# Moving four gate tiles of a two-block transformer kernel into the loop of its recurrent mixer

## The reference, cut to what matters

```python
u = rms_norm_2(h, g_norm_mix[l])
proj = u @ w_in[l] + b_in[l]
mq, mk, mv, mo, mi, mf, nq, nkv, ngate, merge = split_columns(proj, IN_SIZES)
y_m = mlstm_mixer(mq, mk, mv, mo, mi, mf, ...)     # 4 heads x 4 chunks of 128 tokens, recurrent
y_n = nsa_mixer(nq, nkv, ngate, ...)               # compressed, selected and windowed attention
ys = jnp.stack([y_m, y_n], axis=2)
branch = jnp.einsum('btnw,nwd->btnd', ys, w_branch[l])
gates = jax.nn.sigmoid(merge.reshape(B, T, N_BRANCH, D_MODEL))
mixed = jnp.sum(gates * branch, axis=2)            # gate_0 * (y_m @ W_0) + gate_1 * (y_n @ W_1)
h = h + mixed @ w_out[l]
```

## Time and profile before

| | us |
|---|---|
| Time, median of 3 runs (2259.81 to 2261.11) | 2260.12 |
| Profiled execution: its own time | 2263.99 |
| Profiled execution: span of its instructions | 2262.7 |
| TensorE busy, of the span | 2133.4 (94%) |
| VectorE busy | 988.6 (44%) |
| ScalarE busy | 815.3 (36%) |
| GpSimd busy | 226.7 (10%) |
| Mean granted clock of TensorE | 0.979 |

### The profile page before, as it was taken

One profiled execution on the slowest core, in us unless ns is written; L12 is line 12 of the kernel. 1 busy time (PEld: TensorE's weight loads), 2 busy tenths in 40 slices (PEclk: granted clock), 3 DMA queues, 4 the chain that ended last, 5 costly groups with the idle time before them and its releaser, 6 DMA issues. The chain is left out here.

```text
span 2262.7 us, 25574 instructions
## 1 busy us (share of the span) xinstructions
PE 2133.4 (94%) x10364; PEld 1712.6 (76%) x10364; DVE 988.6 (44%) x1833; ACT 815.3 (36%) x1574; POOL 226.7 (10%) x256
## 2 busy tenths in 40 slices
PE   6899899999998999999999999988898999999997
PEld 5667688888887767688888877767665788888886
DVE  6265453323336364453323346645355444333333
ACT  4145443223224355342222334342355434222222
POOL 3003410000000004210000000000254201000000
PEclk9899999999999999999999999989899999999999
DMA  6521123233332312123333222313411232323321
GB/s 154 109 75 57 57 80 106 89 98 103 93 98 71 94 47 75 62 84 97 98 98 93 98 80 75 93 29 84 103 48 38 61 117 84 102 89 101 100 89 69
DMA packets 273721, 192.10 MB, mean 85 GB/s; under 512 B 22060, under 2 KB 241364, under 8 KB 273604
## 3 DMA queue, kind: packets, MB, share of 16 engines
q1 hardware_dynamic: 268704, 177.76, 27.3%
q0 software_dynamic: 4752, 12.67, 2.5%
q10 hardware_dynamic: 148, 0.04, 0.0%
HBM read 186.21 MB, written 4.23 MB: 84 GB/s over the span
## 5 line engine op out<-in xcount | busy, mean ns | idle before, releaser
L584 PE MATMUL bank<-h_features,weights_hi_lo 128*128 128x512 f32 (+1 forms) x5160 | 1138.2, 381 | 17.1 <-DVE weights_hi_lo L917 7.9
L584 PEld LDWEIGHTS bank<-h_features,weights_hi_lo 128*128 128x128 f32 x5160 | 933.7, 190 | 206.7 <-issue 14.6
L917 DVE TENSOR_TENSOR weights_hi_lo<-weights,weights_hi_lo 128x1024 fp32r<-128x1024 f32 (+1 forms) x337 | 402.7, 1199 | 703.7 <-ACT weights_hi_lo L1521 703.1
L1521 ACT ACTIVATE weights_hi_lo<-weights 128x1024 fp32r<-128x1024 f32 (+1 forms) x337 | 340.9, 1016 | 401.2 <-PE bank L626 352.4
L624 PE MATMUL bank<-weights_hi_lo,hidden 128*128 128x512 f32 x528 | 205.4, 389 | 0.0
L625 PE MATMUL bank<-weights_hi_lo,hidden 128*128 128x512 f32 x528 | 205.4, 389 | 0.0
L626 PE MATMUL bank<-weights_hi_lo,hidden 128*128 128x512 f32 x528 | 205.4, 389 | 0.0
L1637 ACT ACTIVATE hidden<-arena 128x512 fp32r<-128x512 f32 x66 | 41.7, 632 | 300.0 <-DVE arena L1068 300.0
L1930 POOL TENSOR_SCALAR arena<-arena,row_stats 128x256 f32<-128x256 f32 (+5 forms) x140 | 126.3, 913 | 198.7 <-DVE row_stats L992 70.9
L1902 POOL TENSOR_TENSOR h_features<-arena,h_features 128x512 fp32r<-128x512 f32 x24 | 30.7, 1278 | 992.0 <-ACT h_features L1549 992.0
L1068 DVE TENSOR_TENSOR arena<-bank,arena 128x512 f32<-128x512 f32 x66 | 45.6, 692 | 181.3 <-PE bank L584 181.3
(11 more groups left out here) (335 smaller groups left out, 2063.8 us busy)
## 6 DMA issues: line engine op xcount, KB each, us to landing
weights<-in_w_in_dram SPq DMA_DIRECT2D x84, 512.0 KB, 3.9
weights<-in_w_gate_dram SPq DMA_DIRECT2D x66, 512.0 KB, 3.8
weights<-in_w_up_dram SPq DMA_DIRECT2D x66, 512.0 KB, 3.8
weights<-in_w_down_dram SPq DMA_DIRECT2D x60, 512.0 KB, 3.6
weights<-in_w_out_dram SPq DMA_DIRECT2D x24, 512.0 KB, 3.7
bias_rows<-decay_scratch POOLq DMA_DIRECT2D x16, 256.0 KB, 4.0
weights<-in_w_cmp_dram SPq DMA_DIRECT2D x16, 256.0 KB, 5.4
weights<-in_w_down_dram SPq DMA_DIRECT2D x12, 256.0 KB, 2.6
```

The costliest lines, as they stand in the source:

```text
L584: last = e.matmul(out_ap, l, r, start=(j == 0), stop=(j == len(pairs) - 1))
L917: e.tensor_tensor(pair_view(i, 1), raw_view(i), pair_view(i, 0).bitcast(F32), ALU.subtract).then_inc(done, tick(("split", i)))
L1521: e.activation(pair_view(i, 0), raw_view(i), ACT.Copy).then_inc(done, tick(("hi", i)))
```

## The change

Gates 0 to 3 are computed inside the recurrent loop, at the end of passes 1, 5, 9 and 13, with their three ScalarE passes at the end of the next pass. Ahead of the compression only branch products 0 and 1 are left. In the attention, branch products 2 to 7 are at steps 3, 11, 19, 27, 35 and 43, gates 4 to 7 at steps 7, 15, 23 and 31; steps 39 and 47 carry nothing. The order of the slabs follows. No tile is added or taken away.

```diff
-GATE_AT = {3 + 8 * i: MERGED_EARLY + i for i in range(ND - MERGED_EARLY)}
-BRANCH_AT = {at + 4: d for at, d in GATE_AT.items()}
+MLSTM_GATE_AT = {1: 0, 5: 1, 9: 2, 13: 3}
+GATE_AT = {7 + 8 * i: len(MLSTM_GATE_AT) + i for i in range(ND - len(MLSTM_GATE_AT))}
+BRANCH_AT = {3 + 8 * i: MERGED_EARLY + i for i in range(ND - MERGED_EARLY)}
+FILLED_AT = sorted([(at, "gate", d) for at, d in GATE_AT.items()] + [(at, "branch", d) for at, d in BRANCH_AT.items()], key=lambda f: (f[0], f[1] == "branch"))
...
-        plan_features(("M", "kv"), w, C_NKV, 384)
+        for i in range(NT * MH):
+            if i in MLSTM_GATE_AT:
+                plan_features(("M", "merge", 0), w, C_MERGE + MLSTM_GATE_AT[i] * P, P)
+            if i in (3, 7, 11):
+                plan_features(("M", "kv"), w, C_NKV + P * (i // 4), P)
...
         for d in range(MERGED_EARLY):
-            plan_merge(0, d)
+            plan_branch(0, d)
...
-        for d in range(MERGED_EARLY, ND):
-            plan_merge(0, d)
+        for _, what, d in FILLED_AT:
+            if what == "gate":
+                plan_features(("M", "merge", 0), w, C_MERGE + d * P, P)
+            else:
+                plan_branch(0, d)
...
   (TensorE, end of pass i of the recurrent loop)
+                    if i in MLSTM_GATE_AT:
+                        feature_tile(("M", "merge", 0, C_MERGE + MLSTM_GATE_AT[i] * P), HT)
                     if i in (3, 7, 11):
                         feature_tile(("M", "kv", C_NKV + P * (i // 4)), HT)
...
   (TensorE, ahead of the compression)
                 for d in range(MERGED_EARLY):
-                    feature_tile(("M", "merge", 0, C_MERGE + d * P), HT)
                     branch(0, d, YM)
...
   (VectorE, end of pass i)
+                    if i in MLSTM_GATE_AT:
+                        splits_for(("M", "merge", 0, C_MERGE + MLSTM_GATE_AT[i] * P))
...
   (ScalarE, end of pass i; first_gate is moved ahead of the loop, unchanged)
+                    if i in MLSTM_GATE_AT:
+                        splits_for(("M", "merge", 0, C_MERGE + MLSTM_GATE_AT[i] * P))
                     if i in (3, 7, 11):
                         kv_tile((KC, VCM, KS)[i // 4], i // 4)
+                    if i - 1 in MLSTM_GATE_AT:
+                        first_gate(MLSTM_GATE_AT[i - 1])
```

More of the change, by code:

```diff
@@ L364, in program, with plan_branch @@
         plan_tokens(("M", "nv"), w, [(C_NKV + 384, C_NKV + 512), (C_NKV + 640, C_NKV + 768)], ND)
-        def plan_merge(n, d):
-            plan_features(("M", "merge", n), w, C_MERGE + D * n + d * P, P)
+        def plan_branch(n, d):
             if n == 0:
@@ L382, in program @@
                                                                     (slice(HD, P), slice(0, P), w1[:, l:l + 8, :])]))
-        for d in range(MERGED_EARLY, ND):
-            plan_merge(0, d)
+        for _, what, d in FILLED_AT:
[3 more added lines that the diff above has]
+                plan_branch(0, d)
         for d in range(ND):
-            plan_merge(1, d)
+            plan_features(("M", "merge", 1), w, C_MERGE + D + d * P, P)
+            plan_branch(1, d)
         for half in range(2):
@@ L1431, in vector_program @@
                 for d in range(MERGED_EARLY):
-                    splits_for(("M", "merge", 0, C_MERGE + d * P))
                     splits_for(("M", "branch", 0, d * P))
@@ L1779, in kv_tile, with first_gate @@
                         banks.leave(act, ("M", "kv", C_NKV + P * col))
+                def first_gate(d):
+                    act.wait_ge(dve.done, dve["neg bias"])
+                    e.activation(FIRST[d], full(("M", "merge", 0, C_MERGE + d * P))[:, :], ACT.Exp, bias=NBM[:, d:d + 1], scale=-1.0
+                                 ).then_inc(done, tick())
+                    banks.leave(act, ("M", "merge", 0, C_MERGE + d * P))
+                    settle()
+                    e.activation(FIRST[d], FIRST[d], ACT.Ln, bias=ONES[:, 0:1]).then_inc(done, tick())
+                    settle()
+                    e.activation(FIRST[d], FIRST[d], ACT.Exp, scale=-1.0).then_inc(done, tick(("M", "merge", 0, d)))
                 for i in range(NT * MH + 2):
@@ L1817, in scalar_program @@
                 slabs_of(("M", "nv"), ND, 256, 1)
[L1819 to L1828, removed]
                 for d in range(MERGED_EARLY):
-                    splits_for(("M", "merge", 0, C_MERGE + d * P))
-                    first_gate(d)
                     splits_for(("M", "branch", 0, d * P))
```

## The result

| | before | after |
|---|---|---|
| Median of the timed runs, us | 2260.61 (4 runs, 2259.81 to 2263.02) | 2244.98 (4 runs, 2241.13 to 2246.47) |
| Ratio to before | | 0.9926, 95% interval 0.9912 to 0.9940 |
| Profiled execution, us | 2263.99 | 2241.13 |

The change makes the kernel 0.74% faster, 16.7 us of 2260.12, give or take 3. The pair of profiles differs by 22.9 us: the execution profiled of the changed kernel was its fastest, the one of before 3 us above its median. So the profiles say in which stage time went, the timed runs how much in all. Of the 22.9 us, 2.8 lie ahead of the recurrent loop, in a part that the change doesn't touch: that is a difference between two executions, not a gain.

The account below looks back on a forecast made before the run. TensorE, busy 94% of the span, bounds the kernel, so only its idle and low-clock time can go. Terms 9.6 - 11.2 + 0.4 - 9.6 = -10.8 us gave 2249.3 us from the 2260.12 median, range 2244 to 2256.

Parts of the forecast that it names:

- The loop: Recurrent loop with its query tiles: four gates, 21.8 us of work, lengthen it by only 9.6 us.
- the loop hides nothing: Rival: waits move behind the loop's gates and the clock still falls; total +1.4 us, 2261.5; chance 0.03.
- uncovered passes: Rival: the gates' ScalarE passes in the loop cause three more 2.1 us waits; total -4.5, 2255.6; chance 0.10.
- The early gates: Stage ahead of the compression: two gates leave and the wait for splits shortens, -11.2 us.
- The compression: Same length expected, plus 0.4 us, since a gate's slab is now split last before the hidden layer's copy.
- The attention: Sum of windows from fill to fill falls from 157.9 to 148.3 us, so -9.6.
- B: Attention window from step 7 to 11 (mod 12), priced 16.03 us with a gate, 12.97 with a product.
- A: Attention window, step 3 to 7 (mod 12): 14.74 us with gate, 10.38 with product; first priced 11.3, unfilled 7.7.
- C: Attention window from step 11 to 3 (mod 12), priced 13.77 us with a gate, 10.34 with a product.
- The attention follows other engines: Rival: step 39 without fill stays 10.38 us, step 43's window stays 16.03; total -5.0, 2255.1; chance 0.16.
- a cold attention: Rival: from step 39 on empty slots drop TensorE's clock until the second branch; +14 us, 2274; chance 0.05.
- More is hidden: Rival: end loses 2.7 us, step 41's wait goes (1.3), query tiles run warm (0.9); -15.7, 2244.4; chance 0.14.

Follow-up runs that it names:

- e4: Changed kernel with gates 0 to 3 at passes 3, 7, 11 and 15 of the loop; ratio to the kernel before 0.9990.
- e8: Changed kernel with gate 3's second and third ScalarE passes moved from the end of pass 14 to behind the loop; ratio to before 0.9914.
- e2: Kernel before with only gates 0 and 1 moved, into loop passes 5 and 9, attention fills as before; ratio to before 0.9943.
- e9: Changed kernel with products 2 and 3 at attention steps 3 and 7, gates 4 to 7 at 11, 19, 27 and 35; ratio to before 0.9927.
- e1: Kernel before with two places of the bank ring skipped behind the attention, no work added; ratio to before 0.9994.
- after_again: The changed kernel, unaltered, run again on the chip of three later experiments; ratio to before 0.9927.
- e10: Changed kernel with gate 0 ahead of pass 0, gate 3's ScalarE passes split, products 2 and 3 at steps 3 and 7, product 7 at 47; ratio to before 0.9898.
- e12: Changed kernel with gates 4 to 7 ahead of the compression, gate 0 before pass 0, gate 3's passes split, product 7 at step 47; ratio to before 0.9867.

## Why the prediction was wrong, step by step

**The loop was right.** Forecast +9.6 with the query tiles; measured +10.3 for the loop and -0.7 for the query tiles (23.56 to 22.86), which is +9.6. Gates 1 and 2 cover the squares, the "kv" tiles behind them take 5.55 to 5.57 us, and the wait at pass 15 is there, 1.6 for a forecast 2. e4 shows that it is the place that does it, e8 that the new wait is ScalarE's passes. Term by term it is 5.0, 0.5, 1.1 and 3.2 for 5.45, 0.6, 1.2 and 2.3, with 0.3 less in between: gate 3 cost 0.9 us more than priced and the rest made up for it. That the sum agrees to the tenth is luck. The case "the loop hides nothing" is out, and that of uncovered passes holds for gate 3 alone, where the 2 us were in the sum.

**The early gates were right.** Forecast -11.2, measured -11.0 and another 0.55 in the wait ahead (6.24 to 5.69). The stage itself took 7.0 to 8.6 us in the kernels that have it, by how long it ran at the lower clock.

**The compression had the wrong sign, by 1.8 us.** Forecast +0.4, measured -1.4. I had put the price on the size of the second slab behind the compression's; what counts is when it has arrived, and the half slab ahead of it brought that forward: e2, with the old order, keeps the old length, and e9 shows the rest of that effect.

**The attention was mis-sized: this is the term that failed.** "New sum: 148.3, old sum 157.9, so -9.6." Measured: -16.8 in the pair, and by means 160.4 (before, e1, e2) against 144.5, -15.9. The sum can be checked window by window. Seven of its twelve came out within 0.13 us, among them B with a gate at step 7 (16.01 for 16.03) and B with a product at step 19 (13.09 for 12.97). Five were shorter than I had priced them: the first A 10.05 for 11.3, B with a gate at step 31 14.75 for 16.03, A without a fill 7.02 for 7.7, B with a product at step 43 11.53 for 12.97, and the end 10.97 for 11.73. Together they are 5.4 us of the miss. The other 1.8 lie outside the windows that I summed: 1.2 at the end (next paragraph), and 0.55 ahead of the first fill, where 1.84 us became 1.29.

The step that failed is that I took each window's length with the clock that it happened to have in the one profile, so the sum has no term for half-clock time that goes away: it gave -9.6, less than the 10.9 us of work that leaves the stage. At steps 31 and 43 alone that is 2.7 us. (Its reason for a gate's extra price, a longer wait for the bank, fits only C, with 0.7 us more idle than with a product; in A and B it is 0.1 and 0.2.) Some of it was chance: in after_again B with a gate at step 31 took 16.01 us, and the first A took 10.6 to 12.8 in the four other executions of this attention. B with a product at step 43 had the full clock in all five. By means and TensorE's busy time (before and e2, which have the bank's wait, against the five), the stage lost 16.2 us: 10.9 of work, 4.4 of busy time that went with the clock, and 0.9 of idle time, in which the bank's 1.5 is gone and 0.6 has come back elsewhere.

**The wait of 1.48 us for bank 7 was missed.** The prediction ended its last window at 1772.27, inside this wait: the old attention ran 1.2 us longer, to 1773.48, and that was not in the old sum.

**The rivals.** "The attention follows other engines" is out at step 43 (B with a product was 11.53, never 16.0) and at step 39 (A without a fill was 7.02, not 10.38), "a cold attention" too: from step 27 on the clock was 1.00. "More is hidden" gave 2244.4, near the truth, but mostly by other terms: the end shrank by 0.8, not 2.7; its warmer query tiles came true (0.7 for 0.9), and A without a fill was 0.7 shorter than forecast for its 1.3. The Trainium skill's page "TensorE: Matmul & The Clock Gate", section "A second HAM failure mode: psum-queue depth-cycling", describes a kernel whose clock oscillates with short idle pieces between groups of matmuls, and windows below the full clock stand in every attention here. What the prediction drew from it, that less filling brings more of them, is not what the means show: the idle time stays at 17 us while the low clock falls from 12.3 to 6.7 and 3.6. The prediction's own reason against it was thin, though: of the windows of the earlier trace rows only A is warmer with a product; B is at 0.87 with a product and 0.89 with a gate, C at 1.00 with either.

**The chances.** The sign had 0.82, rightly. The range's low end was the sum of one rival, and the measured time is 0.6 us beyond it, less than the interval of 3 us can tell. The clock's scatter in the attention alone (4.3 us between five executions of the same program) would have asked for more.

## What to carry to other kernels

Price a movable tile by the wait that it stands on, not by the idle share of the stage: the same four gates cost 10 us at passes 1, 5, 9 and 13 and 28 at 3, 7, 11 and 15. When windows of one profile differ by a clock that dips, take the work at full clock and the dips as terms of their own, and ask a second profile where they fall. Look at what a prefetch in program order stands in front of, and at where a ring of buffers comes to rest behind a stage: both moved time here that no matmul accounts for.

## What the runs showed of the hardware

The half-clock stretches of the attention sit in certain windows, but not in each execution. In the five executions of the changed kernel's attention, the stretch from step 19 to 23 had one each time (13.0 to 13.1 us at 0.87), those from step 7 and from step 15 in two of five, that from step 31 in one, and those from 11, 23, 27, 35, 39 and 43 never. Where one occurs it costs 1.2 to 1.4 us: B with a gate is 14.8 or 16.0, A with a gate 13.3 or 14.7. The time lost to them in the whole attention went from 4.3 to 10.3 us, and the runs of e10 lie 10 us apart, while those of e12, whose attention has two such windows (0.91 and 0.92), lie 4 apart.

What starts one stays open. The waits alone don't tell: here is the same wait of 1.28 us at the same place behind a gate, in one execution of the changed kernel, first at step 7 and then at step 31. Behind the first the six transposes take 1.54 us, behind the second 0.88.

```profile
1626.96 0.70 PE L661 MATMUL bank<-arena 64*128 64x256 f32 x4 [1.28 <-ACT token_scratch L1795]
1627.59 1.54 PE L677 MATMUL bank<-shape_consts,arena 128*128 128x128 f32 x6
```

```profile
1705.20 0.70 PE L661 MATMUL bank<-arena 64*128 64x256 f32 x4 [1.28 <-ACT rotary_scratch L1795]
1705.83 0.88 PE L677 MATMUL bank<-shape_consts,arena 128*128 128x128 f32 x6
```

And in after_again it is the stretch from step 31 that has it:

```profile
1697.13:1713.14 16.01, 14.73 (x74) 9.40 (x72) 7.89 (x36) 8.90 (x28) 9.18 (x9) 0.89 0.06 17
```

Why fewer gates go with fewer of them is open too, and e10, with four gates in other places, had 15.2 us of them in its one profile.
